# The level products of the RWKV triangular inverse on the 32 columns that a level changes

## The reference

```python
def step(state, inp):
    r_t, w_t, k_t, v_t, kk_t, a_t = inp
    sa = jnp.einsum('bhij,bhj->bhi', state, -kk_t)
    state = (state * w_t[:, :, None, :]
             + sa[..., None] * (kk_t * a_t)[:, :, None, :]
             + v_t[..., None] * k_t[:, :, None, :])
    y_t = jnp.einsum('bhij,bhj->bhi', state, r_t)
    return state, y_t
```

## Time and profile before

| | us |
|---|---|
| median of 3 runs | 2474.9 |
| lowest, highest | 2465.89, 2475.51 |
| the profiled execution | 2468.28 |
| its span, first to last instruction | 2466.5 |
| the RWKV stage within it | about 1458 to 1707 |
| the four level loops (i = 0 to 3) | 38.7, 39.4, 40.8, 34.7 |

### The profile page before, as it was taken

One profiled execution on the slowest core, in us unless ns is written; L12 is line 12 of the kernel. 1 busy time (PEld: TensorE's weight loads), 2 busy tenths in 40 slices (PEclk: granted clock), 3 DMA queues, 4 the chain that ended last, 5 costly groups with the idle time before them and its releaser, 6 DMA issues. The chain is left out here.

```text
span 2466.5 us, 39457 instructions
## 1 busy us (share of the span) xinstructions
PE 2345.2 (95%) x16764; PEld 1846.1 (75%) x16764; DVE 1192.4 (48%) x1940; ACT 948.8 (38%) x1388; POOL 819.0 (33%) x369
## 2 busy tenths in 40 slices
PE   7999999998999999999999989987999999999997
PEld 5876677776878857777777778887776678888886
DVE  3354754344133538443431667774454477506434
ACT  5432345434244323453442333332446523212233
POOL 3332233323433412333333332222332244444442
PEclk9999999999999999999999989998999999999999
DMA  4221122122222202222122200001221123223222
GB/s 140 84 90 39 60 77 76 64 66 69 97 77 69 94 26 77 77 69 69 61 91 93 86 27 4 3 4 55 67 67 54 64 97 103 95 97 99 95 95 77
DMA packets 50427, 176.31 MB, mean 71 GB/s; under 512 B 5636, under 2 KB 6604, under 8 KB 50252
## 3 DMA queue, kind: packets, MB, share of 16 engines
q1 hardware_dynamic: 50252, 173.78, 21.4%
HBM read 171.65 MB, written 2.11 MB: 70 GB/s over the span
## 5 line engine op out<-in xcount | busy, mean ns | idle before, releaser
L355 POOL TENSOR_TENSOR w_low<-work,w_high 128x1024 fp32r<-128x1024 f32 x310 | 754.5, 2434 | 1387.5 <-ACT w_high L299 1387.5
L282 PE MATMUL ps<-x_high_tiles,w_high 128*128 128x512 f32 x1640 | 665.9, 406 | 29.9 <-POOL w_low L355 10.6
L282 PE MATMUL ps<-x_low_tiles,w_high 128*128 128x512 f32 x1640 | 644.3, 393 | 2.5 <-DVE x_low_tiles L398 1.7
L282 PE MATMUL ps<-x_high_tiles,w_low 128*128 128x512 f32 x1640 | 644.8, 393 | 0.0
L299 ACT ACTIVATE w_high<-work 128x1024 fp32r<-128x1024 f32 x310 | 327.6, 1057 | 710.6 <-PE ps L282 706.7
L282 PEld LDWEIGHTS ps<-x_high_tiles,w_high 128*128 128x128 f32 x1640 | 311.1, 190 | 138.2 <-issue 60.7
L282 PEld LDWEIGHTS ps<-x_low_tiles,w_high 128*128 128x128 f32 x1640 | 311.2, 190 | 72.4 <-DVE x_low_tiles L398 3.8
L282 PEld LDWEIGHTS ps<-x_high_tiles,w_low 128*128 128x128 f32 x1640 | 311.5, 190 | 67.2 <-issue 5.8
L282 PE MATMUL ps<-arena_parts,w_high 128*128 128x512 f32 x1088 | 346.4, 393 | 13.5 <-POOL w_low L355 5.4
L282 PEld LDWEIGHTS ps<-arena_parts,w_high 128*128 128x128 f32 x1088 | 205.5, 189 | 60.6 <-issue 8.4
L282 PE MATMUL ps<-arena_parts,w_low 128*128 128x512 f32 x544 | 212.9, 391 | 0.0
(11 more groups left out here) (451 smaller groups left out, 2783.3 us busy)
## 6 DMA issues: line engine op xcount, KB each, us to landing
work<-w_first SPq DMA_DIRECT2D x180, 512.0 KB, 3.7
work<-w_second SPq DMA_DIRECT2D x134, 512.0 KB, 3.7
xT_sb<-xT SPq DMA_DIRECT2D x8, 256.0 KB, 4.0
outT<-arena SPq DMA_DIRECT2D x8, 256.0 KB, 2.1
arena<-distance_bias SPq DMA_DIRECT2D x4, 256.0 KB
small<-small SPq DMA_DIRECT2D x1, 819.5 KB, 4.3
arena<-consts SPq DMA_DIRECT2D x1, 544.0 KB, 4.2
base<-consts SPq DMA_DIRECT2D x1, 512.0 KB
```

Source lines behind the costliest of these rows:

```text
L282: ins = pe.matmul(out, lhsT, rhs, start=(n == 0 and k == 0 and q == 0), stop=(n == unit["granules"] - 1 and k == len(ops[i]) - 1 and q == 2))
L355: pool.tensor_tensor(m.wl[:, split_of(g), :], m.raw[:, raw_of(g), :], m.wh[:, split_of(g), :].bitcast(F32), ALU.subtract).then_inc(sem["lo ...
```

## The change

A level changes only half of the columns of a block pair: in `M` one half of each 2b columns (`left`), in `MT` the other (`right`). The edit works on these 32 of every 64 columns.

- `product` takes a selector `half`: the moved operand is the 32 columns of each 64 that the level changes, in runs of b = 2^n columns, and the result goes packed into 256 columns of the bank. The stationary operand stays 64x64, and the number of matmuls is the same.
- ScalarE copies 256 columns and scatters them into the left columns of `T1`. The right columns of `T1` keep what older levels left there.
- VectorE updates the left half of `M` with a subtraction of 256 columns. In the product of `T1` and `MT`, the old columns of `T1` appear as rows of the result that must not count. The update of `MT` is now a `scalar_tensor_tensor`: bank 3 times a factor per row (-1 for rows to be taken, 0 for the others), plus the right half of `MT`.
- These factors are 10 new columns of constants behind the masks; the loaded block of masks grows from 1088 to 1098 columns.
- GpSimd sets both `T1` tiles to zero at the start of the stage, and ScalarE waits for that before its first copy.

```diff
+def blocks_of(x, n):
+    return x.rearrange("q (g two b) -> q g two b", two=2, b=2 ** n)
+def packed(x, n):
+    return x.rearrange("q (g b) -> q g b", b=2 ** n)
...
+    def left(self, x, n):
+        return blocks_of(x, n)[:, :, self.d, :]
+    def right(self, x, n):
+        return blocks_of(x, n)[:, :, 1 - self.d, :]
...
-            def product(w, out, lhsT, rhs):
+            def product(n, out, lhsT, rhs, half):
                 for x in range(NCH):
-                    cols = slice(64 * x, 64 * x + 64)
+                    cols, to = slice(64 * x, 64 * x + 64), slice(32 * x, 32 * x + 32)
                     for p in range(2):
-                        ins = pe.matmul(out[HALF[p], cols], lhsT[HALF[p], cols], rhs[HALF[p], cols], start=True, stop=True)
+                        ins = pe.matmul(packed(out[HALF[p], to], n), lhsT[HALF[p], cols], half(rhs[HALF[p], cols], n), start=True, stop=True)
...
-                        product(w, bank(w, 0), w.L, w.M).then_inc(sem[f"t1_ready{w.d}"], 1)
+                        product(n, bank(w, 0), w.L, w.M, w.left).then_inc(sem[f"t1_ready{w.d}"], 1)
...
-                            product(w, bank(w, 1), w.MT, w.T1).then_inc(sem[f"x_ready{w.d}"], 1)
-                        product(w, bank(w, 3), w.T1, w.MT).then_inc(sem[f"xt_ready{w.d}"], 1)
+                            product(n, bank(w, 1), w.MT, w.T1, w.left).then_inc(sem[f"x_ready{w.d}"], 1)
+                        product(n, bank(w, 3), w.T1, w.MT, w.right).then_inc(sem[f"xt_ready{w.d}"], 1)
...
+                        if i == 0 and n == 1:
+                            act.wait_ge(sem[f"t1_clear{w.d}"], 1)
...
-                        act.activation(w.T1, m.ps[:, w.bank, :], ACT.Copy).then_inc(sem[f"t1_copied{w.d}"], 1)
+                        act.activation(w.left(w.T1, n), packed(m.ps[:, w.bank, 0:256], n), ACT.Copy).then_inc(sem[f"t1_copied{w.d}"], 1)
...
         def _(pool):
+            for w in ways:
+                pool.memset(w.T1, 0.0).then_inc(sem[f"t1_clear{w.d}"], 1)
...
-                            dve.tensor_tensor(w.M, w.M, m.ps[:, w.bank + 1, :], ALU.subtract).then_inc(sem[f"m_ready{w.d}"], 1)
+                            dve.tensor_tensor(w.left(w.M, n), w.left(w.M, n), packed(m.ps[:, w.bank + 1, 0:256], n),
+                                              ALU.subtract).then_inc(sem[f"m_ready{w.d}"], 1)
...
-                        dve.tensor_tensor(w.MT, w.MT, m.ps[:, w.bank + 3, :], ALU.subtract).then_inc(sem[f"mt_ready{w.d}"], 1)
+                        dve.scalar_tensor_tensor(out=w.right(w.MT, n), in0=packed(m.ps[:, w.bank + 3, 0:256], n), scalar=w.rows[:, n - 1:n],
+                                                 in1=w.right(w.MT, n), op0=ALU.mult, op1=ALU.add).then_inc(sem[f"mt_ready{w.d}"], 1)
...
+    even = np.concatenate([(row // b) % 2 == 0 for b in (2, 4, 8, 16, 32)], 1)
+    put("level_rows", -np.concatenate([even, ~even], 1).astype(np.float32))
```

## The result

The changed kernel takes 2540.5 us, the median of 5 runs (2537.6 to 2562.8), against 2470.3 for the kernel before (5 runs, 2465.9 to 2475.5). The ratio is 1.0298, with a 95% interval of 1.0265 to 1.0331: 70 us slower, where 2472 was forecast and the range ended at 2486. The profiled execution is the longest of the five, 2562.8 us with a span of 2561.1.

The account below looks back on a forecast made before the run. TensorE alone was taken to set the level loops' time. Gains of 1.4 + 0.9 + 0.5 = 2.8 us took the profiled 2468.3 to 2465.5 and the median from 2474.9 to 2472; range 2432 to 2486.

Parts of the forecast that it names:

- What bounds the kernel: Stage with the four level loops: TensorE alone sets their time, 153.6 us; VectorE waits for it, one product per 0.93 us.
- What one pair costs: Level products: loading 64 weight columns sets the pace, 57.8 ns per quarter of the array; moving columns overlaps, so halving gains little.
- term (1): The 112 level products move 32 columns, all loads stay: pace 57.8 to 57 ns, gain 1.4 us, ends 0 and 10.4.
- (2): Ends of product groups ahead of transposes or LoRA products: last multiply 25 ns shorter, 36 times, gain 0.9 us.
- Rival A: Level products: pace follows moved columns, a product goes from 0.93 to 0.49 us, net 41 us faster, 2434; chance 0.15.
- (3 to 6): Level loops and stage start: shorter VectorE updates gain 0.5 us at two TensorE waits; copies, memsets and longer constants worth 0.
- rival B: Level loops: granted clock falls to its lower level; all loops low 113 us, priced at a third, 2510; chance 0.06.

Follow-up runs that it names:

- e3: Changed kernel plus 2304 spare load-and-multiply pairs of 64 moved columns in idle quarters of the array, results unpacked and spare ones never read: 2516.1 us, ratio 1.0188.
- e10: Changed kernel, all products at 32 columns, plus 32 spare 64x64 matmuls per pair of heads ahead of the level loops: 2465.4 us, ratio 0.9977.
- e11: Changed kernel with products moving 64 columns again, half updates kept, plus spare matmuls ahead of the level loops: 2466.3 us, ratio 0.9974.
- e2: Changed kernel with four of eight chunks of every product moving 64 columns, four 32 (mean 48), results unpacked: 2470.9 us, ratio 1.0004.
- e1: Changed kernel with products moving all 64 columns again, results unpacked; half copies and updates stay: 2469.5 us, ratio 0.9997.
- e7: Changed kernel with levels 1 and 2 moving all 64 columns, levels 3 to 5 moving 32, results unpacked: 2468.4 us, ratio 0.9999.
- e8: Changed kernel with level 1 alone moving all 64 columns, levels 2 to 5 moving 32, results unpacked: 2466.1 us, ratio 0.9985.
- e9: Changed kernel with only the first product (T1) of level 1 moving 64 columns, all else 32, results unpacked: 2482.9 and 2535.9 us, two runs.
- e4: Changed kernel with all 64 columns moved, in short runs of 2 to 32 columns, half updates kept, results unpacked: 2470.2 us, one run.

## Why the prediction was wrong

**What bounds the kernel**: right. TensorE sets the loops; its busy time is 98 to 100% of theirs at either clock, but for e3.

**What one pair costs**: right. At full clock a product of 32 columns takes what one of 64 takes. Four products are 3.92 us in e10 (above) and 3.95 in e11, where 64 columns are moved:

```profile
1481.18 3.95 PE L1827 MATMUL ps<-work 64*64 64x64 f32 x128
```

and e2's updates are 0.93 us apart. The 128 loads under them take 3.81 us in both, as in the kernel before. So term (1), 1.4 us, came out at 0, its lower end; (2), the shorter end of a group, is the 0.03 us between these two lines, taken as 0.025. Rival A is out.

**Updates, copies, memsets, constants** (3 to 6): right. e1 has 0.9997 with all of them in. The updates took 484 and 420 ns where 451 was taken for both, and TensorE's two waits for a subtraction are gone.

**The clock** is what the forecast had wrong. Its sum, 2.8 us, is worked out at an unchanged clock; the effect of fewer moved columns on the clock was put outside the sum, into rival B, at a chance of 0.06. Rival B named the fall of the clock in the loops, so it had the mechanism. It priced a full fall at 113 us, and 90 came with four lost loops, since parts of each loop stayed at full clock: 219 us at the low clock at 0.43 us each are 94. For the case itself it took a third of that, 2510, where 2540.5 was measured. Two steps led to the 0.06.

The first is the argument against it: the stretch from 1508 to 1525, where the clock stayed 1.00 with columns moving 44% of the time. The 44% counts all 560 multiplies as 64 columns, but 168 of them (L1918 and L1797) move 128; by the same sum it is 728 x 53 / 4 = 9.6 us, 57%. And the row answers another question. It shows work that holds a clock that is up, and e7, e8 and e10 show that products of 32 columns can do that too. Nothing in the row says what happens when they follow a pause, or whether they bring the clock back.

The second is the sentence "One dip more per loop costs some 1.4 us and stays within the forecast". It took over the length of a dip from the kernel before, whose products move 64 columns. There, loops i = 0 and 2 have 0.91 and 0.96: the clock falls 1.4 and 0.8 us into the loop, behind a quiet stretch of up to 2 us, and is back after 7 and 3 us. With 32 columns it is not back until far behind: in loop i = 1 at 1615.3, during line 1874's products ahead of the last level, and in loop i = 0, which has no such products, at 1536.8, during line 1937's behind the loop:

```profile
1614.24 2.06 PE L1874 MATMUL ps<-work,rs 64*64 64x64 f32 x48
```

That those products bring it back is read from their place; no run tested it. A dip that cost 1.4 to 3 us turned into a lost loop of 24. The trace of before held the dips and the products in which they end, and I used them only to price the dip.

The Trainium skill, TensorE: Matmul & The Clock Gate, Part 1 (The HAM clock gate) says that the throttled state is the default and that activity releases it. By that rule the question to ask is the one above, what releases the clock after each quiet stretch. The traces agree for products of 64 columns, behind which the clock is back after 3 to 10 us, and for the filled pause, behind which it is 1.00 in all loops. The page's section Why this matters for your kernels advises to keep TensorE continuously busy. Here TensorE is busy 61.68 of 61.80 us and stays at 1.2 GHz, so for this stream of products the advice, taken by the busy time, doesn't hold, and the measurement decides.

What stays open: why the clock isn't lost in every loop of the same kernel (e9), which property of the thin products matters (columns moved per load, per time, or the share of the array at work), and what the 26 us of idle time in e3 are.

## What to carry to other kernels

Where weight loads set TensorE's pace, moving fewer columns gains nothing, and it can take away the work that keeps the clock up behind a pause and lifts it again. Look for dips of the granted clock in the profile of before, find out which instructions end them, and ask whether the change thins out those. A pause ahead of a long dense stretch can be filled with matmuls nobody reads: 128 of them gave 75 us back here, and 0.26% against the kernel before in e11, where nothing had been slowed.

## What the runs showed of the hardware

- The same work ran at 1.00 or at 0.50 for tens of microseconds with TensorE busy throughout. Levels 3 to 5 with 32 columns kept the clock that they started with in e7 (1.00) and, nearly to their end, in the changed kernel (0.50). In e9 two loops of the same instructions in one execution took 38.7 and 64.3 us.
- The fall came not in the pause but up to 2.7 us behind it, with TensorE busy, in loops i = 0 to 2 of the changed kernel; with the pause filled (e10) it didn't come in any loop.
- At 0.50 a group of 128 pairs of load and multiply took 1.8 times as long, 6.99 to 7.04 us where 3.92 was usual, although at full clock the load and not the multiply set the pace: the loads slow down with the clock (median of one 223 ns in the changed kernel, 135 before).
- Moved operands and results in runs of 2 to 32 float32 columns were as fast as contiguous ones (e4, one run).
- Spare matmuls in the idle quarters of the array left TensorE idle for 26 us for no reason that the profile names (e3).
